# The expert stage of a hybrid encoder step: token gather split into blocks, weight loads reordered, opening split

## The reference

```
xn   = RMSNorm(x);  proj = xn @ w_in            # z | xBC | dt | gate_y | x_lru | g_m | g_r
x   += (sigmoid(g_m) * SSD_branch + sigmoid(g_r) * RGLRU_branch) @ w_o
x   += HierMoE(RMSNorm(x))                      # 4 groups x 8 experts; best group, 2 best experts in it
x   += sigmoid(RMSNorm(x) @ w_ple_gate) * (p @ w_ple)
y    = RMSNorm(x)
expert(xb) = (silu(xb @ w_gate[e]) * (xb @ w_up[e])) @ w_down[e]   # 2048 -> 512 -> 2048
```

## Time and profile before

| what | us |
|---|---|
| median of 3 runs | 2852.29 |
| the profiled execution, its own time | 2848.0 |
| span of its instructions | 2846.5 |
| opening, to the first projection | 0 to 22.9 |
| SSD, LRU, mixing, w_o | 22.9 to 1651 |
| last of w_o, router, gather of the first pair | 1651 to 1683.9 |
| experts, from the first gate product to the end of the last down product | 1683.9 to 2640.5 |
| last stage | 2640.5 to 2846.5 |

### The profile page before, as it was taken

How to read it: one execution, slowest core, us unless ns; L and a number is a source line. 1 busy time by engine, 2 the same in 40 slices (tenths; PEclk the granted TensorE clock), 3 DMA queues, 4 the chain that set the end, 5 groups by cost and what they waited for, 6 DMA issues and landing times.

```text
span 2846.5 us, 39250 instructions
## 1 busy us (share of the span) xinstructions
PE 2716.4 (95%) x16563; PEld 2117.5 (74%) x16563; DVE 928.8 (33%) x1734; ACT 406.8 (14%) x806; POOL 315.7 (11%) x200
## 2 busy tenths in 40 slices
PE   7999999999999999999999979899999999999998
PEld 4666565689999999999998855566555565555687
DVE  3444353558776444544420020111110111101312
ACT  2212120221222000000011110000000000000412
POOL 0000000255656000200010000000000000000000
PEclk9999999999999999999999999999999999999999
DMA  4644344333343333333346259999999999998731
GB/s 147 188 149 130 114 145 127 92 97 108 115 126 111 111 109 114 119 119 119 119 125 243 81 213 413 421 427 426 415 429 417 423 426 423 420 424 360 246 119 45
DMA packets 228075, 637.16 MB, mean 224 GB/s; under 512 B 10316, under 2 KB 199268, under 8 KB 208164
## 3 DMA queue, kind: packets, MB, share of 16 engines
q1 hardware_dynamic: 213840, 605.18, 55.8%
q0 software_dynamic: 10864, 27.57, 3.2%
q10 hardware_dynamic: 3274, 3.01, 0.3%
HBM read 616.18 MB, written 30.04 MB: 227 GB/s over the span
## 4 chain that ended last, share of the span: by engine, by line
PE 84%; DMA 11%; DVE 3%; issue 1%; ACT 1%; SPq 0%; DVEq 0%; POOL 0%; ACTq 0%; POOLq 0%
PE bank L1635 30%; PE bank L1535 15%; DMA arena<-in_w_exp_down_dram 10%; PE bank L1821 9%; PE bank L1806 8%; PE bank L1773 6%; PE bank L1865 6%; PE bank L1733 6%; DMA arena<-in_w_in_dram 1%; PE bank L1779 0%; PE bank L1600 0%; DVE arena L1139 0%; PE bank L1688 0%; PE bank L1687 0%; DMA arena<-expert_rows 0%
## 5 line engine op out<-in xcount | busy, mean ns | idle before, releaser
L1635 PEld LDWEIGHTS bank<-arena 128*128 128x128 f32 x5376 | 876.1, 190 | 10.9 <-issue 6.4
L1635 PE MATMUL bank<-arena 128*128 128x192 f32 x5376 | 878.7, 326 | 5.1 <-issue 4.5
L1806 PE MATMUL bank<-arena 128*64 128x256 f32 x4096 | 450.3, 380 | 9.0 <-DMA arena<-in_w_exp_up_dram 5.2
L1535 PE MATMUL bank<-arena 128*128 128x384 f32 x1280 | 418.2, 489 | 2.5 <-DMA arena<-in_w_in_dram 2.5
L1806 PEld LDWEIGHTS bank<-arena 128*64 128x64 f32 x4096 | 299.8, 137 | 157.6 <-issue 14.1
L1535 PEld LDWEIGHTS bank<-arena 128*128 128x128 f32 x1280 | 243.6, 191 | 174.6 <-issue 5.9
L1821 PE MATMUL bank<-arena 128*64 128x512 f32 x1024 | 245.8, 636 | 45.3 <-DMA arena<-in_w_exp_down_dram 34.4
L1821 PEld LDWEIGHTS bank<-arena 128*64 128x64 f32 x1024 | 77.5, 146 | 193.0 <-issue 193.0
L616 POOL TENSOR_TENSOR arena<-arena 128x1024 f32<-128x1024 f32 x72 | 191.9, 2665 | 153.3 <-DMA arena<-in_w_in_dram 140.1
L1773 PEld LDWEIGHTS bank<-arena 128*128 128x128 f32 x1536 | 174.2, 193 | 17.9 <-issue 17.9
L1773 PE MATMUL bank<-arena 128*128 128x128 f32 x1536 | 177.3, 277 | 5.6 <-issue 5.6
(11 more groups left out here) (339 smaller groups left out, 1651.1 us busy)
## 6 DMA issues: line engine op xcount, KB each, us to landing
arena<-in_w_exp_up_dram SPq DMA_DIRECT2D x32, 4096.0 KB, 17.7
arena<-in_w_exp_down_dram SPq DMA_DIRECT2D x32, 4096.0 KB, 18.3
arena<-in_w_in_dram SPq DMA_DIRECT2D x48, 2048.0 KB, 8.2
arena<-in_w_exp_gate_dram SPq DMA_DIRECT2D x16, 4096.0 KB, 12.3
arena<-in_w_exp_gate_dram SPq DMA_DIRECT2D x32, 2048.0 KB, 17.9
arena<-in_w_out_m_dram SPq DMA_DIRECT2D x8, 2048.0 KB, 8.3
arena<-in_w_out_r_dram SPq DMA_DIRECT2D x8, 2048.0 KB, 8.2
arena<-in_w_o_dram SPq DMA_DIRECT2D x8, 2048.0 KB, 9.2
```

The lines of the kernel that those rows point to most:

```text
L1535: last = mm(banks[(m + c) % 2][:, 0:T], w[:, k, c * 128:(c + 1) * 128], xnT[:, k, :], start=(k == 0), stop=(k == KC - 1))
L1635: last = mm(bank, stationary[:, k, :], moving[:, k, :], start=(k == 0), stop=(k == HK - 1))
L1806: last = mm(banks[2 * x + i][h * SLOTS:(h + 1) * SLOTS, 0:FF // 2], xe[:, k, x * SLOTS:(x + 1) * SLOTS], wk[:, h * (FF // 2):(h + 1) * (FF ...
```

## The change

Four things change.

1. On PE the gather of the next pair is no longer one run between pairs. Its block 0 stands after the up product of the odd expert (where PE waited for DVE's product), block 1 after the transpose of that expert's hidden rows (where PE waited for DVE's copy), blocks 2 and 3 after its down product. The result rows of the pair are computed after the even expert's up product. DVE's order follows: the one-hot matrices of the pair after the next are built at the end of the pair, before the wait for the row indices. The nested loops (passes, pairs) become one loop over all pairs but the last, which is written out; the subtraction of 64 from the ranks moves to each pair's own two columns. The gather of the first pair stands ahead of PE's wait for the number of passes.
2. SP's loads stand in the order in which PE needs them. The odd gate moves behind the down load of the pair before it, the next even gate behind the odd down load. The first pair is written out without the odd gate.
3. In the opening, slab C has its own semaphore, the third tile is transposed into banks 4 to 7, and the B projection runs in two parts, 256 tokens and then 128, waiting for B alone and for the tiles each part needs.
4. POOL's history loads wait for slab B instead of the three tiles of x.

```diff
@@ SP
-            with sp.Fori(0, n_pass * PAIRS - 1) as m:
-                sp.wait_ge(e_step, m * 8 + 5)
-                load_part((m * 2 + 2) % NE, 0)
+            sp.wait_ge(e_step, 5)
+            load_part(2, 0)
+            sp.wait_ge(e_step, 6)
+            load_part(1, 1)
+            sp.wait_ge(e_step, 8)
+            load_part(1, 2)
+            sp.wait_ge(e_step, 10)
+            load_part(2, 1)
+            sp.wait_ge(e_step, 12)
+            load_part(2, 2)
+            with sp.Fori(1, n_pass * PAIRS - 1) as m:
+                sp.wait_ge(e_step, m * 8 + 1)
+                for half in range(2):
+                    load_odd_gate((m * 2 + 1) % NE, half)
                 sp.wait_ge(e_step, m * 8 + 6)
                 load_part((m * 2 + 1) % NE, 1)
                 sp.wait_ge(e_step, m * 8 + 8)
                 load_part((m * 2 + 1) % NE, 2)
-                sp.wait_ge(e_step, m * 8 + 9)
-                for half in range(2):
-                    load_odd_gate((m * 2 + 3) % NE, half)
+                load_part((m * 2 + 2) % NE, 0)
                 sp.wait_ge(e_step, m * 8 + 10)
                 load_part((m * 2 + 2) % NE, 1)
                 sp.wait_ge(e_step, m * 8 + 12)
                 load_part((m * 2 + 2) % NE, 2)
+            for half in range(2):
+                load_odd_gate(NE - 1, half)
             sp.wait_ge(gu_done, n_pass * NE)
             load_part(NE - 1, 1)
...
@@ POOL
-            for t in range(NT):
-                pool.wait_ge(x_loaded[t], 16)
+            pool.wait_ge(side_loaded, 16)
             pool.dma_start(hist_rows[:, 0:XBC], ...
@@ DVE
+            for b in range(4):
+                xe_columns(0, b)
+            dve.wait_ge(rows_mm, 1)
+            next_pick(1, 1)
+            pair_row_indices(0)
+            with dve.Fori(0, n_pass * PAIRS - 1) as n:
+                hidden_product(0, n * 2)
+                hidden_columns(0, n * 2)
+                hidden_product(1, n * 2 + 1)
+                xe_columns(n + 1, 0)
+                hidden_columns(1, n * 2 + 1)
+                for b in range(1, 4):
+                    xe_columns(n + 1, b)
+                dve.wait_ge(rows_mm, n + 2)
+                next_pick(n + 2, (n + 2) % PAIRS)
+                pair_row_indices(n + 1)
@@ PE, opening
             def norm_T(n, src):
                 pe.wait_ge(n_scaled, n + 1)
                 for b in range(4):
-                    pe.wait_ge(n_evac, 4 * n + b + 1)
+                    if n < 2:
+                        pe.wait_ge(n_evac, 4 * n + b + 1)
+                    elif b == 2:
+                        pe.wait_ge(n_rc, 1)
                     for q in range(4):
-                        last = tr(banks[b][...
+                        last = tr(norm_bank(n, b)[...          # bank b, or b + 4 for n == 2
...
+            def by_tokens(w):
+                for tokens, scaled in ((slice(0, SEQ), 4 + 8), (slice(SEQ, T), 4 + 12)):
+                    pe.wait_ge(n_evac, scaled)
+                    for k in range(KC):
+                        last = mm(banks[0][:, tokens], w[:, k, 0:128], xnT[:, k, tokens], start=(k == 0), stop=(k == KC - 1))
+                return last
...
+                        if m + c == 1:
+                            pe.wait_ge(c_or_gain_in, 16 * g + 16)
+                        if m + c == 0 and isinstance(g, int):
+                            last = by_tokens(w)
...
-                pe.wait_ge(side_loaded, 32 * g + 32)
-                if isinstance(g, int):
-                    pe.wait_ge(n_evac, 12 + 4)
+                pe.wait_ge(side_loaded, 16 * g + 16)
                 group_slab(0, slab[2])
@@ PE, experts
             pe.wait_ge(x_sq, 8 * NT)
+            pe.wait_ge(pick_ready, 1)
+            for b in range(4):
+                gather(0, b)
+            result_rows()
 
             pe.wait_ge(pass_ready, 1)
             n_pass = pe.value_load(npass_i[0:1, 0:1], min_val=1, max_val=PASSES)
+            full = pe.value_load(npass_i[0:1, 1:2], min_val=0, max_val=PASSES - 1)
...
+            with pe.Fori(0, n_pass * PAIRS - 1) as n:
+                gate_up(0, n * 2, n)
+                pe.wait_ge(pick_ready, n + 2)
+                pe.wait_ge(rows_ready, n + 1)
+                result_rows()
+                hidden_T(0, n * 2)
+                down(0, n * 2)
+                gate_up(1, n * 2 + 1, n)
+                gather(n + 1, 0)
+                hidden_T(1, n * 2 + 1)
+                gather(n + 1, 1)
+                down(1, n * 2 + 1)
+                for b in (2, 3):
+                    gather(n + 1, b)
+            for x in range(2):
+                E = full * NE + (NE - 2 + x)
+                gate_up(x, E, full * PAIRS + (PAIRS - 1))
+                hidden_T(x, E)
+                down(x, E)
```

More of the change, by code:

```diff
@@ L1418, in _ @@
+            for x in range(2):
+                hidden_product(x, full * NE + (NE - 2 + x))
+                hidden_columns(x, full * NE + (NE - 2 + x))
             dve.wait_ge(r_exp, 1)
@@ new lines, in _, with gate_up @@
+            full = pe.value_load(npass_i[0:1, 1:2], min_val=0, max_val=PASSES - 1)
+            def gate_up(x, E, n):
+                pe.wait_ge(xe_evac, n * 4 + 4 + 2)
+                pe.wait_ge(gu_done, E + 1)
+                for i, w in enumerate((v3(arena[:, GATE_AT:GATE_AT + 2 * SLABF], KC), v3(arena[:, UP_AT:UP_AT + 2 * SLABF], KC))):
+                    odd = (i, x) == (0, 1)
+                    if odd:
+                        pe.wait_ge(odd_loaded, n * 32 + 32)
+                    elif i == 0:
+                        pe.wait_ge(ew_loaded[0], n * 16 + 16)
+                    else:
+                        pe.wait_ge(ew_loaded[1], 16 * E + 16)
+                    for k in range(KC):
+                        wk = gate_odd[k // (KC // 2)][:, k % (KC // 2), :] if odd else w[:, k, :]
+                        for h in range(2):
+                            last = mm(banks[2 * x + i][h * SLOTS:(h + 1) * SLOTS, 0:FF // 2], xe[:, k, x * SLOTS:(x + 1) * SLOTS],
+                                      wk[:, h * (FF // 2):(h + 1) * (FF // 2)], start=(k == 0), stop=(k == KC - 1))
+                    last.then_inc(e_step, 1)
@@ new lines, in hidden_T, with down @@
+            def hidden_T(x, E):
+                pe.wait_ge(h_mul, E + 1)
+                for c in range(2):
+                    last = tr(banks[2 * x + 1][:, FF // 2 + c * 128:FF // 2 + (c + 1) * 128], hrow[x][:, c * 128:(c + 1) * 128], ident)
+                last.then_inc(h_tr, 1)
+            def down(x, E):
+                pe.wait_ge(gu_done, E + 2)
+                pe.wait_ge(ew_loaded[2], 16 * E + 16)
+                wd = v3(arena[:, DOWN_AT:DOWN_AT + 2 * SLABF], FC)
+                for j in range(2):
+                    pe.wait_ge(dn_free, 2 * E + j + 1)
+                    for n in range(FC):
+                        f = (n % 2) * 2 + n // 2
+                        for h in range(2):
+                            last = mm(banks[6 + j][h * SLOTS:(h + 1) * SLOTS, :], hid[x][:, n, :],
+                                      wd[:, f, (2 * h + j) * 512:(2 * h + j + 1) * 512], start=(n == 0), stop=(n == FC - 1))
+                    last.then_inc(e_step, 1)
```

130 lines of the change are left out of this document (38 added, 92 removed).

## The result

The changed kernel takes **2832.9 us** (median of four runs, 2831.95 to 2834.89); the kernel before took 2851.5 beside it (2850.24 to 2853.17). The ratio is 0.9935, interval [0.9918, 0.9953]: 18.6 us, 0.65%, less. The forecast was 2833.6. The profiled execution after was the slowest of its four (2834.9), and that of before (2848.0) was faster than all four runs beside it, so the two traces differ by only 13.1 us. I therefore compare stage by stage.

What follows compares the result with a forecast made beforehand. DMA was taken to bound the expert stage's pairs, PE having 2.7 us to spare. Terms -2.35 - 0.8 - 10.4 - 9.6 + 4.5 = -18.65 took the median from 2852.3 to 2833.6; range 2828 to 2841, widened to 2826 to 2846.

Steps and rivals of the forecast that it cites:

- Steady pairs, DMA: Expert stage: the queue no longer runs dry around the even gate's issue, so the 14 dips go; -10.4 us, bounds 0 and -10.4.
- dips stay: Rival, even gate's issue: the loss is the cost of changing loads, not an empty queue; 2844.0 us, chance 0.18.
- hidden anyway: Rival, expert stage: it keeps its length, only opening and first gather gains stay; 2849.1 us, chance 0.14.
- Steady pairs, PE: Expert stage: filled pauses make PE's pair 56.8 us, 0.9 less, worth nothing by itself as DMA needs 59.6.
- Last pair: End of expert stage: more loads queued, so the rest before expert 31's up load goes; -9.6 us, bounds 0 and -10.5.
- First pairs: Start of expert stage: without the odd gate that filled the queue, gaps appear; +4.5 us, bounds +3 and +6.
- Opening: Kernel start: first projection no longer waits for slab C, starting at 20.45 instead of 22.91; -2.35 us, bounds 0 and -2.5.
- First gather: Before the first gate product: gather starts at 1668.22, not 1670.41; -0.8 us, bounds -2.1 and +0.4.
- PE becomes the bound, slower: Rival, expert stage: gate and up run at half clock in every pair, 63.8 us a pair; 2896 us, chance 0.08.

Runs made afterwards that it cites:

- the run with the old order: The changed kernel with SyncE's old order of loads; PE and DVE keep the new order, the new opening stays: 2832.6 us, ratio 0.9942.

## Why the prediction was right, and where it was not

The time (2833.6 against 2832.9) and the mechanism of the largest terms held; two small terms failed, and one sentence about the cause was wrong.

- **Steady pairs, DMA, -10.4.** Right in size: the middle lost 9.3 us before and 0.1 after, so -9.2; the pairs move 427 GB/s and take 59.85 us for 59.6 foretold, and PE's wait stands ahead of the odd up product. The "dips stay" and "hidden anyway" cases are out.
- **Steady pairs, PE: "worth nothing by itself, as DMA needs ... 59.6".** This sentence failed. I had the two times of the loop side by side (31.6 against 31.9 us) and took them for a queue that is short of 2 us, not for a loop in which PE's gather is one of the links. Moving work out of it brings 8.4 of the 9.3 us alone, as the run with the old order showed (0.9 left in the middle). SyncE's order is a second way to open the same loop, and the two do not add up. The prediction also saw that four of the 14 windows lie above 430 GB/s, and did not ask which: they are the four pairs in which PE's clock had not fallen.
- **Last pair, -9.6.** The transfer loss went from 11.5 to 0.3, more than foretold and more than my bound of 10.5; but PE took some of it back. The last up product ran at low clock behind its wait (9.92 for 7.13), and the last down product no longer waits for a load. The last up load is issued 17.2 us earlier than before, the last down product ends 11.05 earlier. It ends at 2629.42, not near 2622 as foretold; of these 7.6 us, 5.1 were already lost when the stage began (opening and first gather), and 2.5 within it.
- **First pairs, +4.5.** Right: 7.0 lost where 2.8 were, +4.2, with the gaps at 1725 and 1737 as counted.
- **Opening, -2.35.** Right up to 560 us, then worth nothing that can be measured. "From there to the router PE is dense, so that a shift at the opening should pass through" is the step that failed: there are short stops, and their length and the clock behind them change by as much as the shift or more. In the eleven traces with the new opening the long LRU run starts at 883.5 to 885.2 (four), 887.3 to 887.5 (five) and 888.8 to 889.2 (two); in the two with the old one at 887.5 and 887.7. The late seven have a pause of 5.3 to 5.8 us at the LRU's start and 15.9 to 16.1 us for the 80 matmuls behind it, the early four 3.2 to 4.9 and 14.92; the latest two have the 12.18 us for C as well.
- **First gather, -0.8.** Failed: +2.4 in the trace (from the long LRU run to the first gate issue 806.0 us instead of 803.6). I had the start right in what it needs of data and overlooked what the banks wait for (line 1388), so that it came 1.1 us earlier by this count and not 2.2. I took the 12.48 us of the gather as fixed; it took 13.53, as more of it ran at the low clock, and the earlier start was gone at its end. My bound of +0.4 took the register loads for part of the 2.2 us that they had been hidden in: alone in front of the product they cost 1.25 us of stop where 0.26 was, and the fall of the clock behind them 1.5 up to the gate issue. -1.1, +1.05, +1.0 and +1.5 are the +2.4. The fall is not certain: in one of six traces with this program the product ran at full clock, and its gate issue came after 804.0 us.
- **"PE becomes the bound, slower", at clock 0.50 through all of gate and up.** Not seen. The fall behind the wait for the odd up costs 1.6 to 3.0 us (8.72 to 10.11 for 7.13) in six of 14 pairs, and PE had 2.8 us a pair to pay it with.

Against -18.65 foretold, the traces give -0.5 for the opening, +2.4 for the first gather, -13.0 for the expert stage and -2.0 for the last one (1.7 of it in one product that takes 7.14 us instead of 8.83 behind the same pause of 2.74, which the change does not explain): -13.1. Within the stage, 16.2 us less transfer time is lost (-9.2, -11.2, +4.2), and 3.2 are given back; 2.8 of these are the slow up product of the last pair. The medians say -18.6. The 5.5 between traces and medians come from which execution was profiled (a second profile of the changed kernel had a span of 2833.3, where the median was 2830.3), and no step explains them. By the traces the sum is 5.5 us off, and that the forecast fits the median within 0.7 us is therefore partly chance.

## What to carry to other kernels

Where loads and compute both look nearly saturated, follow one buffer around: from the landing of a load through everything the engine does until it frees the next buffer, and through every load queued ahead of the one it waits for. Count the engine's part with the clock that it has behind the loop's own wait: here 26.4 us or 28.1 decided whether the queue ran dry. If that sum is over what the transfers alone need, the loop is the bound, and either taking work out of it (not off the engine) or reordering the loads opens it; do the cheaper one. A load order that runs less far ahead costs one gap when it is entered, one that runs further ahead costs it at the end. And before moving a stage's start, list what its banks wait for, not only its data.

## What the hardware showed that I had not expected

- Two register loads in front of a product cost a stop of 1.25 us, and the granted clock was 0.57 in the 4 us around their end: 1.7 us more. This was so in five of six traces; in the sixth (a stop of 1.22) the product ran at full clock.
- A gather that starts 1.5 us sooner out of an idle stretch ends no sooner: 13.53 us instead of 12.48, at a granted clock of 0.50 in its first window (1668 to 1672).
- PE's waits for a load of 2.2 us are followed by a slow product (8.5 to 8.8 us) in 10 of 14 pairs before and by one of 7.09 in the others: the same wait, the same length. The Trainium skill, TensorE: Matmul & The Clock Gate, section HAM oscillation, tells of a kernel with waits of some 3 to 5 us for DMA in which every burst behind one starts throttled. The waits of 2.2 us here are shorter, and most are followed by a fall all the same; of the 15 waits over 3 us in the two traces of the changed kernel 14 are, and one of 3.23 us is not (7.13).
- The same instructions reach the same point at 883.5 to 889.2 us, by the length of the pause at the LRU's start (3.2 to 5.8 us) and by whether the clock falls behind a few short stops (1.7 us at C, 1.1 at the LRU's start). The 2.5 us gained in the first 20 us of this kernel could not be measured at its end (ratio 1.0003).
